# Neighbourhood attention by pairs of heads: scores in the two row halves of the array, value products alternating between its column halves

## The chip, the cores and the metric

The kernel runs on one core of a Trainium2 chip. The metric is the time of one execution on the device in microseconds. One core has five engines with a queue each: PE (TensorE, matrix products), DVE (VectorE), ACT (ScalarE), POOL (GpSimd) and SP, which issues the transfers. They meet through semaphores alone. PE's array has 128 rows (contraction) and 128 columns (output partitions); a product may use 64 of either.

## What is computed

A trunk of two layers over 512 latent tokens and 256 context tokens, width 1024. The even layer has, between two half feed-forward networks, a multi-scale pooling and a two-dimensional neighbourhood attention of 8 heads of 64, side by side; the odd layer has a recurrent block there. The part that matters here:

```python
def neighbourhood_attention(q, k, v, kc, vc, rpb):
    # q, k, v of the latent tokens on a grid of 8 x 64; kc, vc of the context
    ...
        s_loc = jnp.einsum('bjqhd,bkjchd->bhjqkc', qb, k_slab, preferred_element_type=F32) * NA_SCALE
        ...
        s_loc = jnp.where(mask6, s_loc + bias[None], -jnp.inf)
        s_ctx = jnp.einsum('bjqhd,bmhd->bhjqm', qb, kc, preferred_element_type=F32) * NA_SCALE
        s = jnp.concatenate([s_loc.reshape(B, H, n_cb, NB_COLS, n_loc), s_ctx], axis=-1)
        p = jax.nn.softmax(s, axis=-1).astype(v.dtype)
        ...
        o = (jnp.einsum('bhjqkc,bkjchd->bjqhd', p_loc, v_slab)
             + jnp.einsum('bhjqm,bmhd->bjqhd', p[..., n_loc:], vc))

def context_attention(q, k, v):
    s = jnp.einsum('bqhd,bkhd->bhqk', q, k, preferred_element_type=F32) * NA_SCALE
    p = jax.nn.softmax(s, axis=-1).astype(v.dtype)
    return jnp.einsum('bhqk,bkhd->bqhd', p, v)
```

The latent grid is cut into 4 column blocks of 16 columns. The 128 queries of a block (16 columns of 8 rows) see a slab of 32 columns, 256 keys, and the 256 context keys. The 256 context queries see the context keys.

## The kernel before

Everything is written out engine by engine, in the order in which each engine does it; semaphores count what is done. The attention is in float32, and a float32 product is two records on PE (a high and a low part of the weights); a transpose is one.

**Steps.** `STEPS` lists (h, j): 8 heads, and for each the 4 blocks (j < 4, 512 keys) and 2 tiles of context queries (j = 4, 5, 256 keys), 48 steps. For step s:
- PE `scores(s)` (lines 1799 to 1819): one product, the 128 queries as weights, the keys streaming. A head has 64 channels, so it uses 64 of the 128 rows: head h lies in half h % 2 of tile h // 2 of `q_t` and `k_t`. It writes one bank, half s % 2 of `pair_a`, and waits for `max_done` of step s - 2.
- DVE `lowest(s)` (L1439): adds the bias and takes the row's lowest value into `prob`, buffer s % 3 (scores are kept negated). ACT (L917): the exponential with its row sum. DVE `normalise(s)`: reciprocal (L1447), scaling (L1449).
- PE `turn(s)` (L1829): transposes the 4 (context: 2) tiles of 128 keys into half s % 2 of `pair_b`. ACT `copy_turned(s)` (L852) takes them into `prob_t`, buffer s % 2.
- PE `values(s)` (L1854): 4 (context: 2) products with 64 columns of values as weights, summed in `pair_c` (blocks) or `pair_r` (context queries), in the partitions of half h % 2 and in bank (h // 2) % 2, so that two pairs of heads have their own outputs.
- When both heads of pair t are done, DVE `take_heads(t)` (L1458, L1460) copies the 768 outputs to `mixed`, ACT `heads_high` (L911) and POOL `heads_low` (L676) split them into a high and a low part for the output projection, which is the next stage.

**Order.** PE: scores 0 and 1, and then in turn scores(s + 2), turn(s), values(s - 1). DVE: lowest(s), normalise(s - 1), and take_heads(t) in step j = 3 of the head after next. ACT: exponential(s), copy_turned(s - 1). POOL makes three bias tiles for a head (L692) in buffer h % 2, once the head two before no longer reads them, from tables which SP loads (L578).

The loop on PE, whose order stays:

```python
            scores(0)
            scores(1)
            for s in range(n):
                if s + 2 < n:
                    scores(s + 2)
                turn(s)
                if s >= 1:
                    values(s - 1)
            values(n - 1)
```

## Time and profile before

| | us |
|---|---|
| median of 3 runs | 2909.53 (2909.39 to 2911.92) |
| profiled execution | 2915.29 |
| its span, first to last instruction | 2913.5 |
| attention in it, first score product to first load of the next stage | 118.0 (831.24 to 949.20) |

The profile is of one execution. The windows of rows 2 leave out the first one, from 831.24 to 837.26; their sum row holds all three. A row of a timeline gives the start and how long the group lasts to the end of its last instruction, which overlaps the next one's start. Since products are pipelined, their own durations are latencies: what one costs PE is read from the distance between the starts of weight loads ("PEld"). A product over 64 rows reads 64\*128, one that makes 64 columns 128\*64. "issue" in brackets means that the engine waited for nothing but its own queue.

### The profile page before, as it was taken

Reading aid. Unit: us, or ns where it says so; the run is one execution under the profiler, and the core shown is the slowest. Engines: PE = TensorE matmul, PEld = TensorE weight load, DVE = VectorE, ACT = ScalarE, POOL = GpSimd, SP = SyncE. Lnnn points to the kernel's source line nnn. Section 1 sums busy time; section 2 is a strip of 40 time slices with the busy share of each in tenths; the row PEclk is TensorE's granted clock in tenths of the full one; section 3 lists DMA queues with packets and bytes.
Section 4 is the critical chain, followed back from the end, with each engine's and each line's share of the span. In section 5 each row is a group of like instructions: output and inputs, shape, how many; then the busy total and the mean of one; then the engine's idle time right before and its main releaser. Section 6 shows DMA issues by size and latency. Waiting matters only on the chain.

```text
span 2913.5 us, 40217 instructions
## 1 busy us (share of the span) xinstructions
PE 2767.8 (95%) x15161; PEld 2597.9 (89%) x15161; DVE 1485.7 (51%) x2553; ACT 772.6 (27%) x1039; POOL 896.8 (31%) x360
## 2 busy tenths in 40 slices
PE   6799999999999989999999999999998887899998
PEld 6799999998965989999999899999997775778887
DVE  5655555655535366655665523522238887432233
ACT  1322111112145232211111322111125665332222
POOL 0133222332222223322332223222223444244442
PEclk6899999999999999999999999999998997999999
DMA  5244334432210234434443122312211112223332
GB/s 197 58 127 129 111 101 126 127 100 69 68 61 19 65 88 115 123 100 116 115 123 107 44 65 80 107 58 61 75 52 40 55 54 57 70 86 107 88 101 79
DMA packets 413083, 256.77 MB, mean 88 GB/s; under 512 B 6653, under 2 KB 405846, under 8 KB 413014
## 3 DMA queue, kind: packets, MB, share of 16 engines
q1 hardware_dynamic: 413014, 255.87, 30.4%
q8 instruction: 40, 0.66, 0.1%
q14 instruction: 29, 0.24, 0.0%
HBM read 252.70 MB, written 4.25 MB: 88 GB/s over the span
## 4 chain that ended last, share of the span: by engine, by line
PE 65%; issue 19%; DVE 6%; POOL 5%; ACT 4%; DMA 0%; SPq 0%; POOLq 0%; DVEq 0%; ACTq 0%
PE pair_b L1575 28%; PE pair_a L1575 28%; POOL w_lo L647 5%; PE pair_c L1625 2%; PE pair_c L1854 1%; PE pair_a L1815 1%; DVE decay L1535 1%; PE pair_b L1829 1%; DVE decay L1533 1%; PE pair_a L1565 1%; DVE gate_i L1529 1%; DVE h_lo L1176 1%; DVE root L1527 1%; ACT decay L975 1%; ACT root L977 1%
## 5 line engine op out<-in xcount | busy, mean ns | idle before, releaser
L647 POOL TENSOR_TENSOR w_lo<-raw,w_hi 128x1024 fp32r<-128x1024 f32 (+3 forms) x302 | 829.5, 2748 | 1796.7 <-ACT w_hi L750 1796.7
L750 ACT ACTIVATE w_hi<-raw 128x1024 fp32r<-128x1024 f32 (+3 forms) x302 | 337.2, 1117 | 1281.1 <-PE pair_b L1575 443.7
L1067 DVE TENSOR_TENSOR work_g<-work_s,pair_b 128x768 f32<-128x768 f32 (+1 forms) x88 | 78.1, 888 | 702.2 <-PE pair_b L1575 539.7
L1037 DVE SCALAR_TENSOR_TENSOR ada_sums<-ada_raw,cvec,ada_sums 128x256 f32<-128x256 f32 x896 | 395.7, 515 | 0.0
L1575 PE MATMUL pair_a<-h_hi,w_hi 128*128 128x384 f32 x1312 | 338.3, 338 | 9.6 <-POOL w_lo L647 9.6
L1575 PE MATMUL pair_a<-h_lo,w_hi 128*128 128x384 f32 x1312 | 333.6, 335 | 0.0
L1575 PE MATMUL pair_a<-h_hi,w_lo 128*128 128x384 f32 x1312 | 333.6, 335 | 0.0
L1575 PE MATMUL pair_b<-h_hi,w_hi 128*128 128x384 f32 x1168 | 297.7, 335 | 5.9 <-POOL w_lo L647 5.9
L1575 PE MATMUL pair_b<-h_hi,w_lo 128*128 128x384 f32 x1168 | 297.6, 335 | 0.0
L1575 PE MATMUL pair_b<-h_lo,w_hi 128*128 128x384 f32 x1168 | 297.5, 335 | 0.0
L1575 PEld LDWEIGHTS pair_a<-h_hi,w_hi 128*128 128x128 f32 x1312 | 234.5, 189 | 13.5 <-issue 9.6
L1575 PEld LDWEIGHTS pair_a<-h_lo,w_hi 128*128 128x128 f32 x1312 | 237.5, 188 | 0.0
L1575 PEld LDWEIGHTS pair_a<-h_hi,w_lo 128*128 128x128 f32 x1312 | 237.5, 188 | 0.0
L1575 PEld LDWEIGHTS pair_b<-h_hi,w_hi 128*128 128x128 f32 x1168 | 211.7, 189 | 6.5 <-POOL w_lo L647 6.5
L1575 PEld LDWEIGHTS pair_b<-h_lo,w_hi 128*128 128x128 f32 x1168 | 211.9, 189 | 0.0
L1575 PEld LDWEIGHTS pair_b<-h_hi,w_lo 128*128 128x128 f32 x1168 | 211.9, 189 | 0.0
L1098 DVE SCALAR_TENSOR_TENSOR resid<-pair_b,mod_g,resid 128x512 f32<-128x512 f32 (+3 forms) x74 | 42.3, 603 | 314.4 <-PE pair_b L1575 245.2
L1565 PE MATMUL pair_b<-h_hi,w_hi 128*128 128x512 f32 (+3 forms) x352 | 140.0, 398 | 33.3 <-DVE gelu L1514 33.1
L1073 DVE TENSOR_TENSOR g_lo<-work_g,g_hi 128x768 f32 (+1 forms) x88 | 147.3, 1673 | 10.8
L1566 PE MATMUL pair_b<-h_lo,w_hi 128*128 128x512 f32 (+3 forms) x352 | 137.5, 391 | 0.0
L1565 PE MATMUL pair_a<-h_hi,w_hi 128*128 128x512 f32 (+2 forms) x280 | 115.7, 413 | 22.8 <-DVE h_lo L1176 19.2
L1567 PE MATMUL pair_b<-h_hi,w_lo 128*128 128x512 f32 (+3 forms) x352 | 136.8, 389 | 0.0
(272 smaller groups left out, 4548.5 us busy)
## 6 DMA issues: line engine op xcount, KB each, us to landing
raw<-in_ffn_w_gu_dram SPq DMA_DIRECT2D x176, 512.0 KB, 3.9
ada_raw<-in_ada_w_dram SPq DMA_DIRECT2D x64, 1024.0 KB, 5.2
raw<-in_ffn_w_down_dram SPq DMA_DIRECT2D x64, 704.0 KB, 5.5
raw<-in_rg_w_in_dram SPq DMA_DIRECT2D x20, 512.0 KB, 3.8
ada_first<-in_ada_w_dram SPq DMA_DIRECT2D x4, 2048.0 KB, 18.0
raw<-in_ab_w_in_dram SPq DMA_DIRECT2D x16, 512.0 KB, 3.8
raw<-in_rg_w_out_dram SPq DMA_DIRECT2D x8, 640.0 KB, 4.6
raw<-in_ab_w_out_dram SPq DMA_DIRECT2D x8, 512.0 KB, 4.1
```

The lines of the kernel that those rows point to most:

```text
L647: nc.gpsimd.tensor_tensor(wl[:, par, 0:kt * P], raw[:, par, 0:kt * P], wh[:, par, 0:kt * P].bitcast(F32), ALU.subtract).then_inc(split_rea ...
L750: nc.scalar.activation(wh[:, par, 0:kt * P], raw[:, par, 0:kt * P], ACT.Copy).then_inc(hi_done, 1)
L975: nc.scalar.activation(decay[d][:, :], gate_r[d][:, :], ACT.Exp, bias=rg_scale[:, m:m + 1], scale=rg_scale[:, m:m + 1])
L1037: step = nc.vector.scalar_tensor_tensor(out=sums[v], in0=tiles(k), scalar=c_k, in1=sums[v], op0=ALU.mult, op1=ALU.add)
L1067: nc.vector.tensor_tensor(gbuf[:, 0, 0:W], sbuf[:, 0, 0:W], up, ALU.mult)\
L1073: nc.vector.tensor_tensor(gl[:, ds(i, 1), 0:W].rearrange("p o n -> p (o n)"), gbuf[:, 0, 0:W], gh[:, ds(i, 1), 0:W].rearrange("p o n -> p ...
L1098: return nc.vector.scalar_tensor_tensor(out=resid[:, k, a:b], in0=src, scalar=mod_g[:, SITE[name], k, v:v + 1], in1=resid[:, k, a:b], op0= ...
L1565: nc.tensor.matmul(dst, w1, hi, start=start, stop=False)
L1566: nc.tensor.matmul(dst, w1, lo, start=False, stop=False)
L1567: return nc.tensor.matmul(dst, w2, hi, start=False, stop=stop)
L1575: last = nc.tensor.matmul(tokens(ps, a, a + HALF), w, of[:, k, a:a + HALF], start=begins, stop=ends)
L1625: last = nc.tensor.matmul(pC[:, 2 * t + v:2 * t + v + 1], ada_sum[:, v, t * P:(t + 1) * P], ones[:, 0:1], start=True, stop=True)
```

## The change

`STEPS` becomes 24 steps of (t, j), where t is a pair of heads. Each step does both heads a = 0, 1:
- scores: head 0's product in rows 0 to 63, then head 1's in rows 64 to 127, to the two halves of one double bank; double banks `pair_a` and `pair_b` alternate.
- turns: both heads' tiles, now to `pair_c`, half a. prob has 6 buffers, prob_t and `pair_c` one for each head, so turn(s, a) waits for copy(s - 1, a), and copy(s, a) for values(s - 1).
- values: for each tile of keys head 0's product and then head 1's, to partitions 0 to 63 and 64 to 127 of `pair_r`, blocks in its first bank and context queries in its second. There is one set of outputs: the first values of a pair wait for `heads_taken` of the pair before.
- DVE does lowest for both heads, then normalise for both of the step before; take_heads comes in the second step of the next pair (j == 1). ACT does two exponentials, then two copies; heads_high comes in the third step.
- POOL makes the bias tiles variant by variant for both heads, each as soon as the pair before no longer reads that variant.

```diff
-        prob = late("prob", [P, 3, 512])
+        prob = late("prob", [P, 3 * 2, 512])
...
-        STEPS = [(h, j) for h in range(HEADS) for j in range(BLOCKS + 2)]
+        STEPS = [(t, j) for t in range(KP) for j in range(BLOCKS + 2)]
+        PER_PAIR = BLOCKS + 2
+        def keys_of(j):
+            return NK + CTX if j < BLOCKS else CTX
+        def nth(s, a):
+            return 2 * s + a + 1
+        def stat(tile, s, a):
+            n = s % 4 * 2 + a
+            return tile[:, n:n + 1]
...
-                    sp.wait_ge(bias_done, h - 1)
+                    sp.wait_ge(bias_done, 3 * (h // 2))
...
-            for h in range(HEADS):
-                if h == 2:
+            def biases(t, v):
+                if v == 0:
+                    for a in range(2):
+                        pool.wait_ge(table_landed[a], 16 * (t + 1))
+                if t >= 1:
+                    last_use = max(j for j in range(BLOCKS) if VARIANT[j] == v)
+                    pool.wait_ge(max_done, nth(PER_PAIR * (t - 1) + last_use, 1))
+                for a in range(2):
+                    shifted = bass.AP(tensor=table[:, :, :].tensor, offset=table[:, a, SHIFT[v]:SHIFT[v] + 1].offset,
+                                      ap=[list(table[:, 0, 0:1].ap[0]), [1, SLAB], [RPB_C, GRID_R]])
+                    last = nc.gpsimd.tensor_tensor(bias[:, 3 * a + v, :].rearrange("p (c r) -> p c r", r=GRID_R),
+                                                   mask[:, v, :].rearrange("p (c r) -> p c r", r=GRID_R), shifted, ALU.subtract)
+                last.then_inc(bias_done, 1)
+            pool.wait_ge(mask_done, 1)
+            for t in range(KP):
+                if t == 1:
                     low(P_ABOUT, 0, KD)
                     low(P_ABOUT + 1, 1, KD)
-                pool.wait_ge(table_landed[h % 2], 16 * (h // 2 + 1))
-                pool.wait_ge(mask_done, 1)
-                if h >= 2:
-                    pool.wait_ge(max_done, (BLOCKS + 2) * (h - 2) + BLOCKS)
                 for v in range(3):
-                    t = bass.AP(tensor=table[:, :, :].tensor, offset=table[:, h % 2, SHIFT[v]:SHIFT[v] + 1].offset,
-                                ap=[list(table[:, 0, 0:1].ap[0]), [1, SLAB], [RPB_C, GRID_R]])
-                    last = nc.gpsimd.tensor_tensor(bias[:, h % 2 * 3 + v, :].rearrange("p (c r) -> p c r", r=GRID_R),
-                                                   mask[:, v, :].rearrange("p (c r) -> p c r", r=GRID_R), t, ALU.subtract)
-                last.then_inc(bias_done, 1)
-                if h in (3, 5, 7):
-                    heads_low(h // 2 - 1)
+                    biases(t, v)
+                if t >= 1:
+                    heads_low(t - 1)
...
-            def copy_turned(s):
-                j, b = STEPS[s][1], s % 2
-                W = NK + CTX if j < BLOCKS else CTX
-                act.wait_ge(turned_done, s + 1)
-                if s >= 2:
-                    act.wait_ge(pv_done, s - 1)
-                nc.scalar.activation(prob_t[:, b, 0:W], pB[:, b * 512:b * 512 + W], ACT.Copy).then_inc(prob_t_done, 1)
+            def copy_turned(s, a):
+                W = keys_of(STEPS[s][1])
+                act.wait_ge(turned_done, nth(s, a))
+                if s >= 1:
+                    act.wait_ge(pv_done, s)
+                nc.scalar.activation(prob_t[:, a, 0:W], pC[:, a * 512:a * 512 + W], ACT.Copy).then_inc(prob_t_done, 1)
...
-                if j == 5 and h % 2 == 0 and h >= 2:
-                    heads_high(h // 2 - 1)
-            copy_turned(len(STEPS) - 1)
+                    for a in range(2):
+                        copy_turned(s - 1, a)
+                if j == 2 and t >= 1:
+                    heads_high(t - 1)
+            for a in range(2):
+                copy_turned(len(STEPS) - 1, a)
...
             def take_heads(t):
-                dve.wait_ge(pv_done, (2 * t + 2) * (BLOCKS + 2))
+                dve.wait_ge(pv_done, PER_PAIR * (t + 1))
                 dve.wait_ge(mixed_split, KP + t - 1)
                 f = att_f[:, t % 2, :]
-                o, oc = pC[:, (t % 2) * 512:(t % 2) * 512 + SEQ], pR[:, (t % 2) * 512:(t % 2) * 512 + CTX]
+                o, oc = pR[:, 0:SEQ], pR[:, 512:512 + CTX]
...
-            for s, (h, j) in enumerate(STEPS):
-                lowest(s)
+            for s, (t, j) in enumerate(STEPS):
+                for a in range(2):
+                    lowest(s, a)
                 if s >= 1:
-                    normalise(s - 1)
-                if j == 3 and h % 2 == 0 and h >= 2:
-                    take_heads(h // 2 - 1)
-            normalise(len(STEPS) - 1)
+                    for a in range(2):
+                        normalise(s - 1, a)
+                if j == 1 and t >= 1:
+                    take_heads(t - 1)
+            for a in range(2):
+                normalise(len(STEPS) - 1, a)
...
             def scores(s):
-                h, j = STEPS[s]
-                t, a = divmod(h, 2)
-                rows = slice(a * DH, (a + 1) * DH)
-                b = s % 2
-                if s >= 2:
-                    pe.wait_ge(max_done, s - 1)
+                t, j = STEPS[s]
+                if s < 2:
+                    pe.wait_ge(proj_done, 2 + 16)
+                for a in range(2):
+                    rows = slice(a * DH, (a + 1) * DH)
+                    if s >= 2:
+                        pe.wait_ge(max_done, nth(s - 2, a))
+                    bank = pair[s % 2][:, a * 512:(a + 1) * 512]
+                    if j < BLOCKS:
+                        q = qT[rows, t, (BLOCKS - 1 - j) * P:(BLOCKS - j) * P]
+                        k0 = SLAB_AT[j] * GRID_R
+                        keys = bass.AP(tensor=kT[:, :, :].tensor, offset=kT[rows, t, k0:k0 + 1].offset,
+                                       ap=[list(kT[rows, t, 0:1].ap[0]), [SEQ - k0, 2], [1, NK]])
+                        bank = bank.rearrange("p (g n) -> p g n", n=NK)
+                    else:
+                        q, keys, bank = qT[rows, t, j * P:(j + 1) * P], kT[rows, t, SEQ:T], bank[:, 0:CTX]
+                    nc.tensor.matmul(bank, q, keys, start=True, stop=True).then_inc(scores_done, 1)
+            def turn(s, a):
+                pe.wait_ge(prob_scaled, nth(s, a))
+                if s == 0:
+                    pe.wait_ge(mixed_done, KP)
                 else:
-                    pe.wait_ge(proj_done, 2 + 16)
-                bank = pA[:, b * 512:(b + 1) * 512]
-                if j < BLOCKS:
-                    q = qT[rows, t, (BLOCKS - 1 - j) * P:(BLOCKS - j) * P]
-                    k0 = SLAB_AT[j] * GRID_R
-                    keys = bass.AP(tensor=kT[:, :, :].tensor, offset=kT[rows, t, k0:k0 + 1].offset,
-                                   ap=[list(kT[rows, t, 0:1].ap[0]), [SEQ - k0, 2], [1, NK]])
-                    last = nc.tensor.matmul(bank[:, :].rearrange("p (g n) -> p g n", n=NK), q, keys, start=True, stop=True)
-                else:
-                    q = qT[rows, t, j * P:(j + 1) * P]
-                    last = nc.tensor.matmul(bank[:, 0:CTX], q, kT[rows, t, SEQ:T], start=True, stop=True)
-                last.then_inc(scores_done, 1)
-            def turn(s):
-                h, j = STEPS[s]
-                b = s % 2
-                pe.wait_ge(prob_scaled, s + 1)
-                if s >= 2:
-                    pe.wait_ge(prob_t_done, s - 1)
-                for t in range(4 if j < BLOCKS else 2):
-                    last = nc.tensor.transpose(pB[:, b * 512 + t * P:b * 512 + (t + 1) * P],
-                                               prob[:, s % 3, t * P:(t + 1) * P], ident[:, :])
+                    pe.wait_ge(prob_t_done, nth(s - 1, a))
+                for i in range(keys_of(STEPS[s][1]) // P):
+                    last = nc.tensor.transpose(pC[:, a * 512 + i * P:a * 512 + (i + 1) * P],
+                                               prob[:, s % 3 * 2 + a, i * P:(i + 1) * P], ident[:, :])
                 last.then_inc(turned_done, 1)
             def values(s):
-                h, j = STEPS[s]
-                t, a = divmod(h, 2)
-                rows = slice(a * DH, (a + 1) * DH)
-                b = s % 2
-                pe.wait_ge(prob_t_done, s + 1)
+                t, j = STEPS[s]
+                pe.wait_ge(prob_t_done, nth(s, 1))
                 if s == 0:
                     pe.wait_ge(v_loaded, 16 * BLOCKS)
-                    pe.wait_ge(mixed_done, KP)
-                if j == 0 and a == 0 and t >= 2:
-                    pe.wait_ge(heads_taken, t - 1)
-                if j < BLOCKS:
-                    c0 = (t % 2) * 512 + (BLOCKS - 1 - j) * P
-                    dst = pC[rows, c0:c0 + P]
-                    tiles = [vslab[:, 2 * j, h * DH:(h + 1) * DH], vslab[:, 2 * j + 1, h * DH:(h + 1) * DH]]
-                else:
-                    dst = pR[rows, (t % 2) * 512 + (j - BLOCKS) * P:(t % 2) * 512 + (j - BLOCKS + 1) * P]
-                    tiles = []
-                tiles += [vtok[:, SEQ // P + i, h * DH:(h + 1) * DH] for i in range(2)]
+                if j == 0 and t >= 1:
+                    pe.wait_ge(heads_taken, t)
+                c0 = (BLOCKS - 1 - j) * P if j < BLOCKS else 512 + (j - BLOCKS) * P
+                tiles = [vslab[:, 2 * j, :], vslab[:, 2 * j + 1, :]] if j < BLOCKS else []
+                tiles += [vtok[:, SEQ // P + i, :] for i in range(2)]
                 for i, v in enumerate(tiles):
-                    last = nc.tensor.matmul(dst, v, prob_t[:, b, i * P:(i + 1) * P], start=(i == 0),
-                                            stop=(i == len(tiles) - 1))
+                    for a in range(2):
+                        h = 2 * t + a
+                        last = nc.tensor.matmul(pR[a * DH:(a + 1) * DH, c0:c0 + P], v[:, h * DH:(h + 1) * DH],
+                                                prob_t[:, a, i * P:(i + 1) * P], start=(i == 0), stop=(i == len(tiles) - 1))
                 last.then_inc(pv_done, 1)
...
-                turn(s)
+                for a in range(2):
+                    turn(s, a)
                 if s >= 1:
                     values(s - 1)
```

PE, a context step's turns and values between two block steps' scores, before (one head; names with buffer numbers, ident_63 is the identity, pair_a the score banks, pair_b the turned, pair_r and pair_c the outputs):

```order
L1815 MATMUL pair_a<-k_t_83,q_t_82 128x512 [waits max_done]
L1829 MATMUL pair_b<-ident_63,prob_85 128x128 [waits prob_t_done,prob_scaled]
L1829 MATMUL pair_b<-ident_63,prob_85 128x128
L1854 MATMUL pair_r<-prob_t_88,v_tokens_80 64x128 [waits prob_t_done]
L1854 MATMUL pair_r<-prob_t_88,v_tokens_80 64x128
L1815 MATMUL pair_a<-k_t_83,q_t_82 128x512 [waits max_done]
```

and after, the same place of the second pair:

```order
L1840 MATMUL pair_b<-k_t_83,q_t_82 128x512 [waits max_done] x2
L1849 MATMUL pair_c<-ident_63,prob_85 128x128 [waits prob_t_done,prob_scaled]
L1849 MATMUL pair_c<-ident_63,prob_85 128x128
L1849 MATMUL pair_c<-ident_63,prob_85 128x128 [waits prob_t_done,prob_scaled]
L1849 MATMUL pair_c<-ident_63,prob_85 128x128
L1867 MATMUL pair_r<-prob_t_88,v_tokens_80 64x128 [waits prob_t_done]
L1867 MATMUL pair_r<-prob_t_88,v_tokens_80 64x128 x3
L1840 MATMUL pair_a<-k_t_83,q_t_82 128x512 [waits max_done] x2
```

Every shape now comes twice in a row, once for each head, and only then does PE go to the next shape.

DVE around the copies of a finished pair's outputs, before (ISA is `lowest`):

```order
L1439 ISA prob,neg_max<-pair_a,bias 128x512 [waits scores_done,turned_done]
L1439 ISA neg_max 128x1
L1447 RECIPROCAL row_inv<-row_sum 128x1 [waits prob_done]
L1449 TENSOR_SCALAR prob<-prob,row_inv 128x512 [waits inv_done]
L1458 COPY mixed<-pair_c 128x512 [waits mixed_split,pv_done]
L1460 COPY mixed<-pair_r 128x256
L1439 ISA prob,neg_max<-pair_a,bias 128x256 [waits scores_done,turned_done]
L1439 ISA neg_max 128x1
```

and after:

```order
L1467 RECIPROCAL row_inv<-row_sum 128x1 [waits prob_done]
L1469 TENSOR_SCALAR prob<-prob,row_inv 128x512 [waits inv_done]
L1478 COPY mixed<-pair_r 128x512 [waits mixed_split,pv_done]
L1480 COPY mixed<-pair_r 128x256
L1460 ISA prob,neg_max<-pair_a,bias 128x512 [waits scores_done,turned_done,bias_done]
L1460 ISA neg_max 128x1
L1460 ISA prob,neg_max<-pair_a,bias 128x512 [waits scores_done,turned_done,bias_done]
L1460 ISA neg_max 128x1
L1467 RECIPROCAL row_inv<-row_sum 128x1 [waits prob_done]
L1469 TENSOR_SCALAR prob<-prob,row_inv 128x512 [waits inv_done]
```

The copies moved from the fourth step of the head after next to the second step of the next pair, right behind the last values that they wait for; two lowest and two scalings are queued behind them.

## Rows read from the trace of the kernel before

**Rows 1.** The page's busy times: us, share of the span, instructions.
```profile
PE 2767.8 (95%) x15161; PEld 2597.9 (89%) x15161; DVE 1485.7 (51%) x2553; ACT 772.6 (27%) x1039; POOL 896.8 (31%) x360
```

**Rows 2.** Windows: length, busy PE, PEld, DVE, ACT, POOL, granted clock, DMA.
```profile
837.26:847.50 10.24, 10.24 (x33) 6.44 (x33) 3.17 (x12) 3.68 (x9) 2.75 (x3) 0.50 0.05 14
847.50:949.20 101.70, 101.47 (x538) 59.70 (x537) 55.65 (x180) 53.80 (x134) 19.00 (x18) 1.00 0.06 15
sum 117.96, PE 115.01 PEld 67.29 DVE 63.13 ACT 62.83 POOL 21.75; mean PE 38.34 PEld 22.43 DVE 21.04 ACT 20.94 POOL 7.25
```

**Rows 3.** Timeline of PE's weight loads, one head: start, length, instruction.
```profile
863.25 0.29 PEld L1815 LDWEIGHTS pair_a<-k_t,q_t 64*128 64x128 f32 x2 [0.17 <-issue]
864.30 0.20 PEld L1829 LDWEIGHTS pair_b<-ident,prob 128*128 128x128 f32 x2 [0.76 <-issue]
864.67 0.41 PEld L1854 LDWEIGHTS pair_c<-prob_t,v_slabs 128*64 128x64 f32 x4 [0.17 <-issue]
...
868.74 0.42 PEld L1829 LDWEIGHTS pair_b<-ident,prob 128*128 128x128 f32 x4 [0.76 <-DVE prob L1449]
869.33 0.41 PEld L1854 LDWEIGHTS pair_r<-prob_t,v_tokens 128*64 128x64 f32 x4 [0.17 <-issue]
869.91 0.29 PEld L1815 LDWEIGHTS pair_a<-k_t,q_t 64*128 64x128 f32 x2 [0.17 <-issue]
...
871.55 0.41 PEld L1854 LDWEIGHTS pair_c<-prob_t,v_slabs 128*64 128x64 f32 x4 [0.17 <-issue]
...
872.57 0.29 PEld L1818 LDWEIGHTS pair_a<-k_t,q_t 64*128 64x128 f32 x2 [0.17 <-issue]
873.19 0.42 PEld L1829 LDWEIGHTS pair_b<-ident,prob 128*128 128x128 f32 x4 [0.33 <-issue]
...
877.03 0.18 PEld L1815 LDWEIGHTS pair_a<-k_t,q_t 64*128 64x128 f32 x1 [0.17 <-issue]
```

**Rows 4.** Timeline of the start, all engines.
```profile
831.24 1.98 PE L1815 MATMUL pair_a<-k_t,q_t 64*128 64x512 f32 x4
...
834.75 0.68 DVE L1439 CUSTOM_DVE_ANT_1 prob<-pair_a,bias 128x512 f32<-128x512 f32 x1
835.36 0.08 DVE L1439 DVE_READ_ACCUMULATOR2_ANT neg_max<- 128x1 f32 x1
...
835.50 1.12 PE L1815 MATMUL pair_a<-k_t,q_t 64*128 64x512 f32 x2 [2.28 <-DVE neg_max L1439]
...
836.33 0.16 DVE L1447 RECIPROCAL row_inv<-row_sum 128x1 f32<-128x1 f32 x1 [0.27 <-ACT prob L917]
836.53 0.49 DVE L1449 TENSOR_SCALAR prob<-prob,row_inv 128x512 f32<-128x512 f32 x1
...
837.07 0.98 PE L1829 MATMUL pair_b<-ident,prob 128*128 128x128 f32 x4 [0.45 <-DVE prob L1449]
```

**Rows 5.** Weight loads of value products: the first two together, and min/median/max ns.
```profile
862.23 0.19 PEld L1854 LDWEIGHTS pair_c<-prob_t,v_slabs 128*64 128x64 f32 x2 [0.17 <-issue]
...
L1854 PEld LDWEIGHTS pair_c<-prob_t,v_slabs x128: 132/137/231, 841.0 to 947.0; 128*64 128x64 f32 x128
```

**Rows 6.** Groups by form, 834 to 950: busy us, mean ns of one, idle before.
```profile
L917 ACT ACTIVATE prob<-prob,neg_max 128x512 f32<-128x512 f32 x32 | 22.9, 716 | 1.5 <-DVE neg_max L1439 0.3
...
L852 ACT ACTIVATE prob_t<-pair_b 128x512 f32<-128x512 f32 x32 | 19.1, 598 | 35.8 <-PE pair_b L1829 35.8
...
L676 POOL TENSOR_TENSOR h_lo<-mixed,h_hi 128x768 fp32r<-128x768 f32 x3 | 5.4, 1813 | 56.1 <-ACT h_hi L911 56.1
...
L1458 DVE COPY mixed<-pair_c 128x512 f32<-128x512 f32 x4 | 2.7, 686 | 2.2 <-PE pair_r L1854 2.2
...
L1460 DVE COPY mixed<-pair_r 128x256 f32<-128x256 f32 x4 | 1.7, 416 | 0.0
```

**Rows 7.** Timeline where POOL makes bias tiles beside a scaling.
```profile
881.52 2.67 POOL L692 TENSOR_TENSOR bias<-mask,rpb_table 128x256 f32<-128x256 f32 x3
881.56 1.10 DVE L1449 TENSOR_SCALAR prob<-prob,row_inv 128x512 f32<-128x512 f32 x1
```

56 lines of the change are left out of this document (27 added, 29 removed).

## The prediction

> **What bounds the kernel now.** I read first the page's busy shares, then the windows of the attention stage, then the weight loads of one head in it, the timeline of its start, and its groups by form. PE is busy for 95% of the span [rows 1]. The change touches one stage alone: from the first score product at 831.24 to the first load of the output projection at 949.20, 118.0 us, in which PE is busy 115.0, DVE 63.1 and ACT 62.8 us [rows 2]. Before and behind it nothing moves, so its gain or loss is that of the kernel as long as the stage behind finds its weights split and its heads ready, which I come to.
>
> In the steady part PE sets the pace. A head takes 877.03 - 863.25 = 13.78 us [rows 3]. Read the distances between loads: a block's scores 1.05 (863.25 to 864.30), a context block's 0.62 (872.57 to 873.19), four turns 0.59 (868.74 to 869.33), two turns 0.37 (864.30 to 864.67), eight value records 1.02 (871.55 to 872.57), four 0.58 (869.33 to 869.91) [rows 3]. With 4 blocks and 2 context blocks a head: 4 x (1.05 + 0.59 + 1.02) + 2 x (0.62 + 0.37 + 0.58) = 13.78. The head is PE's own work to the last 0.01 us; eight heads are 110.2. The other 7.8 us of 118.0 are the start (below).
>
> (2) The halves. Head 0's scores are followed by head 1's in the other rows and another bank, and value products go to alternating column halves. Before, neighbours are always in one half, so no row shows whether two halves stream at once. Bounds: not at all (0.43 and 0.11 each, as now), or as far as two records of one half can't overlap. In the order a-high, a-low, b-high, b-low the second of head 0 and the first of head 1 then run together: 3 times instead of 4 for a pair of scores, and 2k+1 instead of 4k for k tiles of values. I take the full overlap: the operands, the output banks or partitions and the weights are all disjoint, and two 64-column loads with the product between them start 0.055 apart [rows 5], so issue and loading can feed a record every 0.055 us. Nearest rows for a gain are those of one half, which is the other end of the range.
>
> The Trainium skill, "TensorEngine Tiling (Array Packing)", section Key Properties, says that tiles load and multiply in parallel and that only a change of mode drains the array; by it I would take this same end, and by the rows alone either. The Trainium skill, "TensorE: Matmul & The Clock Gate", Part 3, says on the other hand that a load overlaps running matmuls only when its row group differs. Value products all use all rows, so by it the loads would be exposed. This trace speaks against it: eight value records come at 0.11 us each with their loads hidden [rows 3]. If it held between column halves, two overlapped records would cost 0.11 + 2 x 0.055 = 0.22, as much as now, and only the scores would gain.
>
> With full overlap a block step is scores 0.19 + 3 x 0.43 = 1.48, turns 0.15 + 8 x 0.11 = 1.03, values 0.14 + 9 x 0.11 = 1.13: 3.64. A context step is 0.84 + 0.59 + 0.69 = 2.12. A pair: 4 x 3.64 + 2 x 2.12 = 18.8, four pairs 75.2 us, where 110.2 stood.
>
> (3) Do DVE and ACT keep up? Per block step DVE does for two heads lowest 0.61 (834.75 to 835.36), reciprocal and scaling 0.20 + 0.49 (836.33 to 837.02): 2.6 us; ACT two exponentials at 0.72 and two copies at 0.60: 2.6 [rows 4, 6]. Both are below 3.64, and a context step needs about 1.7 of 2.12. Copies: the turned bank and prob_t are now single, so turn(s, a) waits for copy(s-1, a), which waits for values(s-2). While PE does scores (1.48), the first copy (0.60 and a hand-over of 0.1) ends; at context scores (0.84) by 0.1 us only. Free, but without slack.
>
> (4) The new wait. pair_r now holds one pair's outputs instead of two. take_heads stands in DVE's order behind normalise(6t+6) and waits for the last values of pair t. Behind it are queued lowest(6t+8), both heads, and normalise(6t+7), for which PE's turn(6t+7) waits. From the end of those values: 0.1 + 1.10 for the two copies [rows 6] + 1.22 for two lowest + 0.69 = 3.1; PE meanwhile has only the next scores, 1.48. A wait of 1.6, with an echo of 0.1, at three boundaries: 5.1 us. Before, take_heads came steps later and hid.
>
> (5) The end: after the last scores nothing covers the chain. The two copies after values(22) stand bare (0.9), and the last two context steps' exponentials and scalings, now two heads deep, cost some 1.6: 2.5 us.
>
> (6) The start. Scores 0 wait in the bank until DVE comes free at 834.75; turn 0 came at 837.07. Now four lowest stand ahead: 834.75 + 4 x 0.61 + 0.69 = 837.9. Against the same schedule without that delay this is 1.9 us. Then the clock: after PE's waits of 2.28 and 0.45 [rows 4] the granted clock was 0.50 for 10.24 us [rows 2], the lower level, 1.2 GHz of 2.4; with PE bound that costs 5.1. With overlap PE waits about as long (until 835.5, and from 837.1 to 837.9), so I keep 5.1.
>
> (7) POOL. Bias tiles are the same 24, asked for variant by variant. While three of them run (2.67), a scaling takes 1.10 [rows 7] instead of 0.49 [rows 4], and PE's next turn is behind it. With less slack I add 1.5, two or three such cases. Order: once heads_high has ended, in a pair's third step, heads_low (1.81) and the first variant's two tiles (2 x 0.9) [rows 6, 7] take 3.6, and by the step times above the next pair's first lowest comes some 5 us after; free, and if not it costs 1 or 2 us a pair. SP's table loads wait for bias tiles of a pair earlier and have a whole pair's time. Behind the stage the last heads take the same chain, and the POOL splits of the next panels follow it as before: nothing.
>
> **Sum**: 75.2 + 5.1 + 2.5 + 1.9 + 5.1 + 1.5 = 91.3 against 118.0: 26.7 us less. The profiled execution took 2915.29 (span 2913.5), which becomes 2888.6; the median of the runs, 5.76 lower, 2909.53, becomes 2882.8. If the clock holds at the start, 2877.7.
>
> **Rivals.**
> A. *Halves take turns.* Against it only the disjointness; for it, that no row shows two products at once. A block step is 1.91 + 1.03 + 1.90 = 4.84, a context step 2.66: a pair 24.7, all 98.7. Plus boundaries 3 x 1.3, end 2.5, start 1.0, POOL 0.5, and 0 to 5.1 of clock: 106.6 to 111.7, so 2898 to 2903; 2900.5.
> B. *Overlap in part*: the load of the other half starts only when the first half's last record does, or values gain nothing (the rule above), or the bare hand-overs of (3) cost 0.3 to 0.5 a step. A scores pair 1.59, a four-tile couple of values 0.32 instead of 0.22 a tile: a pair 21.3, 10 us more than the forecast in all; values without gain give 15 more. 2888 to 2898; 2893.
> C. *Each change of half drains, as a change of shape does*, 0.145 a time. There are 7 in a block's values, 3 in a context block's and 1 in scores: 16 x 7 + 8 x 3 + 24 = 160, so 23 us on top of A: 2921 to 2926, slower; 2923. It turns the sign from 0.04 to 0.07 us a change on. For it: the drain of 0.09 in every fixed part. Against: it comes with a new shape, and here the shape stays.
> D. *The pairs don't change PE's bound*: some other new wait in DVE, POOL or the tables eats the gain of A; within 5 us of 2909.5.
>
> **How the numbers follow.** Forecast 0.46, A 0.22, B 0.21, C 0.07, D 0.04. About 0.2%, 5.8 us, is what a measurement can tell here. Faster: the forecast, B and nine tenths of A, 0.87; the same: the slow end of A and most of D, 0.05; slower: C and a little of D, 0.08. The range of eight in ten, 2876 to 2903, holds the forecast with the clock held or fallen, B and A.
>
> **What would show it.** Scores: four records whose second and third start together and a group of 1.48, not 1.91. Values: 16 records in 1.13, not 1.90 (0.055 or 0.11 apart), or 2.9 under C. A pair of 18.8 plus one wait at a boundary, PE's turn waiting for DVE's scaling behind the two mixed copies. The clock at 0.50 for some 10 us near 837. Wrong would be a wait in every step for copies or scalings, a lowest waiting for bias, or a gain that shows in the stage and not in the span.

## The result and the profile after

| | before | after |
|---|---|---|
| median of 4 runs | 2910.31 (2909.39 to 2911.92) | 2877.55 (2877.28 to 2879.45) |
| profiled execution | 2915.29 | 2877.64 |
| its span | 2913.5 | 2875.9 |
| attention in it | 117.96 (831.24 to 949.20) | 84.63 (828.51 to 913.14) |

The ratio of the times is 0.9889, with a 95% interval of 0.9873 to 0.9905: 1.1% faster, 32.8 us between the medians. The two profiled executions differ by 37.7: 33.3 in the attention stage, 2.7 ahead of it and 1.6 behind it. What lies ahead of the stage took 828.5 us after and 831.2 before, what lies behind it 1962.7 and 1964.3. Over all executions below these two are 826.2 to 833.6 and 1960.6 to 1964.0, whatever stands in the stage, so totals of single executions scatter by some us, and the length of the stage is the better measure.

The page's busy times of after, beside [rows 1]:

```profile
PE 2719.7 (95%) x15161; PEld 2569.5 (89%) x15161; DVE 1487.4 (52%) x2553; ACT 768.7 (27%) x1039; POOL 891.1 (31%) x360
```

PE is busy 48 us less with the same 15161 instructions. DVE, ACT and POOL are within 6 us of what they were. The windows of the stage, columns as in [rows 2]:

```profile
828.51:833.40 4.89, 2.62 (x12) 1.00 (x11) 3.48 (x8) 4.47 (x7) 0.00 (x0) 1.00 0.00 0
833.40:840.22 6.82, 6.77 (x20) 3.36 (x19) 6.50 (x17) 4.88 (x14) 3.52 (x4) 0.50 0.01 4
840.22:913.14 72.92, 61.52 (x550) 38.44 (x548) 53.99 (x178) 49.78 (x133) 18.11 (x17) 1.00 0.08 23
sum 84.63, PE 70.91 PEld 42.81 DVE 63.96 ACT 59.13 POOL 21.63; mean PE 23.64 PEld 14.27 DVE 21.32 ACT 19.71 POOL 7.21
```

PE had been busy for 115.0 of 118.0 us; now it is for 70.9 of 84.6, and DVE, at 64.0, is not far from it. The part at a granted clock of 0.50 is 6.8 us instead of 10.24.

A step with block scores, a context step's turns and block values: weight loads on PE, with the product row of its scores last (compare [rows 3]):

```profile
847.83 0.30 PEld L1840 LDWEIGHTS pair_a<-k_t,q_t 64*128 64x128 f32 x4 [0.17 <-issue]
848.89 0.52 PEld L1849 LDWEIGHTS pair_c<-ident,prob 128*128 128x128 f32 x4 [0.76 <-issue]
849.57 0.42 PEld L1867 LDWEIGHTS pair_r<-prob_t,v_slabs 128*64 128x64 f32 x8 [0.17 <-issue]
849.96 0.47 PEld L1867 LDWEIGHTS pair_r<-prob_t,v_tokens 128*64 128x64 f32 x8
850.60 0.30 PEld L1840 LDWEIGHTS pair_b<-k_t,q_t 64*128 64x128 f32 x4 [0.17 <-DVE neg_max L1460]
...
847.83 1.13 PE L1840 MATMUL pair_a<-k_t,q_t 64*128 64x512 f32 x4
```

The four loads of two heads' scores take 0.30 us, and the next shape follows 1.06 behind the first (847.83 to 848.89). One head alone took 1.05. So two block products cost what one did: the halves overlap not in part but wholly. Values: 16 records from 849.57 to 850.60 in 1.03, where 8 took 1.02. (The turns between them are those of a context step: 849.57 - 848.89 = 0.68, of which four turns are 0.59, and 0.09 is a wait.)

The boundary of a pair, PE's weight loads:

```profile
855.62 0.30 PEld L1840 LDWEIGHTS pair_b<-k_t,q_t 64*128 64x128 f32 x4 [0.17 <-issue]
858.63 0.42 PEld L1849 LDWEIGHTS pair_c<-ident,prob 128*128 128x128 f32 x4 [2.71 <-DVE prob L1469]
...
860.84 0.30 PEld L1840 LDWEIGHTS pair_a<-k_t,q_t 64*128 64x128 f32 x4 [0.17 <-issue]
861.73 0.91 PEld L1849 LDWEIGHTS pair_c<-ident,prob 128*128 128x128 f32 x8 [0.59 <-DVE prob L1469]
863.83 0.30 PEld L1840 LDWEIGHTS pair_b<-k_t,q_t 64*128 64x128 f32 x4 [0.17 <-issue]
865.07 0.42 PEld L1849 LDWEIGHTS pair_c<-ident,prob 128*128 128x128 f32 x4 [0.94 <-DVE prob L1469]
...
867.69 0.30 PEld L1840 LDWEIGHTS pair_a<-k_t,q_t 64*128 64x128 f32 x4 [0.17 <-issue]
...
875.49 0.30 PEld L1840 LDWEIGHTS pair_b<-k_t,q_t 64*128 64x128 f32 x4 [0.17 <-issue]
...
903.54 0.30 PEld L1840 LDWEIGHTS pair_b<-k_t,q_t 64*128 64x128 f32 x4 [0.17 <-issue]
```

and the other engines there:

```profile
855.75 0.69 DVE L1478 COPY mixed<-pair_r 128x512 f32<-128x512 f32 x1 [1.35 <-PE pair_r L1867]
...
861.01 1.09 ACT L872 ACTIVATE prob_t<-pair_c 128x512 f32<-128x512 f32 x2 [2.09 <-PE pair_r L1867]
...
861.99 0.84 ACT L931 ACTIVATE h_hi<-mixed 128x768 fp32r<-128x768 f32 x1
...
862.91 1.82 POOL L690 TENSOR_TENSOR h_lo<-mixed,h_hi 128x768 fp32r<-128x768 f32 x1 [20.02 <-ACT h_hi L931]
863.57 0.16 DVE L1467 RECIPROCAL row_inv<-row_sum 128x1 f32<-128x1 f32 x1 [1.10 <-ACT prob L938]
863.76 1.25 DVE L1469 TENSOR_SCALAR prob<-prob,row_inv 128x512 f32<-128x512 f32 x1
```

At the start of the stage, DVE's first `lowest` and the first of its rows there with idle time:

```profile
832.02 0.68 DVE L1460 CUSTOM_DVE_ANT_1 prob<-pair_a,bias 128x512 f32<-128x512 f32 x1
...
839.65 0.69 DVE L1460 CUSTOM_DVE_ANT_1 prob<-pair_b,bias 128x512 f32<-128x512 f32 x1 [0.18 <-PE pair_b L1840]
```

Between the two it works without a pause, and PE waits for it (2.27 us ahead of scores 2 at 832.77). Now the steady part. A step is the stretch from one scores' load to the next, named by the turns in it; the boundary is that of a pair's second step. A pair takes 19.87 us (855.62 to 875.49) and the next one 19.85, 19.86 on average. PE's own work for a pair, from distances between loads in which nothing is waited for, is 4 x 3.10 + 2 x 1.79 = 15.98, where 3.10 is 1.05 + 1.03 + 1.03 but for rounding and 1.79 is 0.62 + 0.59 + 0.58. So a pair holds 3.88 of waits. DVE stands idle 1.35 for the last values of a pair, copies them, and only then does the two lowest and the scaling that PE's turn waits for: this step takes 5.22 (855.62 to 860.84; 5.21 at the next two boundaries) instead of 3.10. The third takes 2.99 (860.84 to 863.83) instead of 0.62 + 1.03 + 1.03 = 2.68: turns wait for the copies out of the single bank. (The row of the turns at 861.73 names DVE's scaling, but head 0's had ended at 860.99; the first of ACT's two copies, which began at 861.01, ends some 0.1 ahead of the turns.) The fourth takes 3.86 (863.83 to 867.69) instead of 2.68: ACT does heads_high (0.84) ahead of the exponentials, DVE's reciprocal waits 1.10 for them, and the scaling behind it, for which PE's turns wait, takes 1.25 instead of 0.49 while POOL runs heads_low. The rest, 0.26, lies in three steps.

### The profile page after: what moved, and what is told of

Same layout as the page of the kernel before. It is cut to its first block, busy times and chain, and to the rows that moved or that the text cites. A ratio compares the mean times of both kernels' runs of the same rounds, so it can differ in the third digit from the quotient of the medians.

```text
span 2875.9 us, 40218 instructions
## 1 busy us (share of the span) xinstructions
PE 2719.7 (95%) x15161; PEld 2569.5 (89%) x15161; DVE 1487.4 (52%) x2553; ACT 768.7 (27%) x1039; POOL 891.1 (31%) x360
## 4 chain that ended last, share of the span: by engine, by line
PE 64%; issue 20%; DVE 7%; POOL 5%; ACT 4%; DMA 0%; SPq 0%; POOLq 0%; DVEq 0%; ACTq 0%
PE pair_b L1598 29%; PE pair_a L1598 28%; POOL w_lo L661 5%; PE pair_c L1648 2%; DVE decay L1558 1%; DVE decay L1556 1%; DVE h_lo L1199 1%; PE pair_c L1849 1%; DVE gate_i L1552 1%; PE pair_a L1588 1%; DVE root L1550 1%; ACT root L1000 1%; ACT decay L998 1%; DVE ada_sums L1060 1%; PE pair_r L1867 1%
## 5 line engine op out<-in xcount | busy, mean ns | idle before, releaser
L1096 DVE TENSOR_TENSOR g_lo<-work_g,g_hi 128x768 f32 (+1 forms) x88 | 161.5, 1835 | 10.8
## 6 DMA issues: line engine op xcount, KB each, us to landing
ada_first<-in_ada_w_dram SPq DMA_DIRECT2D x4, 2048.0 KB, 17.9
```

The source lines that it names most:

```text
L1096: nc.vector.tensor_tensor(gl[:, ds(i, 1), 0:W].rearrange("p o n -> p (o n)"), gbuf[:, 0, 0:W], gh[:, ds(i, 1), 0:W].rearrange("p o n -> p ...
```

## The experiments

Unless one says otherwise, a kernel is the changed one with the edit shown. "Stage" is the time from the first score load to the first load of the next stage. The half-clock stretches (granted clock 0.50, TensorE at 1.2 GHz) inside it are given with it, since they differ between executions of one kernel.

| kernel | time, median | before, same chip | stage | stretches at 0.50 |
|---|---|---|---|---|
| changed | 2877.55 | 2910.31 | 84.6 | 6.8 at the start |
| changed, again (e12) | 2880.41 | 2911.46 | 86.5 | 6.8 start, 3.4 last boundary |
| values by head (e1) | 2883.04 | 2910.12 | 93.6 | 6.8 start, 3.4 at two boundaries |
| scores in one half (e2) | 2890.61 | 2910.12 | 94.9 | 10.2 start |
| values in one half (e3) | 2897.10 | 2910.12 | 101.6 | 3.4 start, 3.4 at two boundaries |
| both in one half (e4) | 2905.98 | 2910.12 | 106.9 | none |
| the same, again (e11) | 2903.76 | 2911.46 | 111.3 | 3.4 at three boundaries |
| copies a step later (e5) | 2872.20 | 2910.67 | 78.6 | 3.4 start |
| no bias tiles (e6) | 2877.18 | 2910.67 | 87.0 | 6.8 start, 3.4 at two boundaries |
| both of these (e8) | 2874.97 | 2910.67 | 78.4 | 6.8 start |
| filler at the start (e7) | 2878.13 | 2910.67 | 85.3 | 3.4 last boundary |
| later, heads_high in step 5, bias tiles first (e9) | 2877.43 | 2911.46 | 82.4 | 3.4 start |
| later, heads_high in step 4 (e10) | 2875.42 | 2909.50 | 79.6 | 6.8 start |

The medians are of ten runs for "both in one half", of four where a ratio stands below, and else one run. The four runs of "changed, again" lie 5.3 us apart, so single runs that differ by less are not told apart by their times; there the steps of the trace carry the argument.

### Do the halves stream at once?

Three kernels keep the order and the waits of the change and take away one thing, the halves. *Scores in one half* (e2):

```diff
-                    rows = slice(a * DH, (a + 1) * DH)
+                    rows = slice(0, DH)
```

> The changed kernel, with both heads' score products taken from head 0's 64 rows (head 1's scores are head 0's, so head 1 is not computed). Theory, only the difference of rows lets the two run together: four records of a block step go from 1.05 to 0.19 + 4 x 0.43 = 1.91 us, context ones from 0.62 to 1.05; a pair's own work goes up by 4 x 0.86 + 2 x 0.43 = 4.3, less what it covers of the wait at the boundary and for scalings: the stage 92 to 98 from 84.6. Rival, the different banks are enough: no change.

Weight loads of one pair of block scores:

```profile
852.47 0.29 PEld L1840 LDWEIGHTS pair_a<-k_t,q_t 64*128 64x128 f32 x2 [0.17 <-issue]
853.01 0.19 PEld L1840 LDWEIGHTS pair_a<-k_t,q_t 64*128 64x128 f32 x1 [0.24 <-issue]
853.44 0.19 PEld L1840 LDWEIGHTS pair_a<-k_t,q_t 64*128 64x128 f32 x1 [0.24 <-issue]
854.38 0.42 PEld L1849 LDWEIGHTS pair_c<-ident,prob 128*128 128x128 f32 x4 [0.76 <-issue]
```

The four loads are now 0.43 apart from the second on, and the group lasts 1.91 (852.47 to 854.38), the price for no overlap; with two halves it was 1.06. Nothing but the rows differs.

*Values in one half* (e3):

```diff
-                        last = nc.tensor.matmul(pR[a * DH:(a + 1) * DH, c0:c0 + P], v[:, h * DH:(h + 1) * DH],
-                                                prob_t[:, a, i * P:(i + 1) * P], start=(i == 0), stop=(i == len(tiles) - 1))
+                        last = nc.tensor.matmul(pR[0:DH, c0:c0 + P], v[:, h * DH:(h + 1) * DH],
+                                                prob_t[:, a, i * P:(i + 1) * P], start=(i == 0 and a == 0),
+                                                stop=(i == len(tiles) - 1 and a == 1))
```

> The changed kernel, with both heads' value products summed into partitions 0 to 63 (the outputs of the two heads are added and the upper half is not computed). Theory, only the difference of column halves lets them run together: a block's 16 value records go from 1.03 to 0.14 + 16 x 0.11 = 1.90 us, a context step's 8 from 0.58 to 1.02; a pair 4 x 0.87 + 2 x 0.44 = 4.4 longer, less what it hides of waits: the stage 94 to 101. Rival: no change.

```profile
847.80 0.85 PEld L1867 LDWEIGHTS pair_r<-prob_t,v_slabs 128*64 128x64 f32 x8 [0.17 <-issue]
...
849.70 0.30 PEld L1840 LDWEIGHTS pair_b<-k_t,q_t 64*128 64x128 f32 x4 [0.17 <-issue]
```

Sixteen records take 1.90 (847.80 to 849.70) instead of 1.03. The stage of 101.6 lies just above the expected 94 to 101; its clock fell at two boundaries, which took 7.61 and 7.58 where the third took 6.07. Both edits at once (e4), and the same kernel once more (e11):

> The changed kernel with both of these: scores of both heads from head 0's rows, values of both into partitions 0 to 63 (so head 1 is not computed and the outputs are added). What is left of the change is that both heads are done behind each other in each shape of the array: half the changes of shape, and the waits of the single buffers. By the steps of the prediction (rival A): a pair 24.7, the stage 106 to 112, the kernel 2898 to 2903. If changes of shape cost nothing: a pair 27.6 as before, and slower than before by the boundary waits, 2912 to 2918.

> e4 once more, for a second trace: its first profiled execution had the stage at 106.9 with the clock at 1.00 throughout, while its timed runs spread from 2899 to 2912. Theory: the spread comes from whether the clock falls in the waits of the start and of the boundaries, which here costs PE time, because PE is the bound: the same step times (a pair 25.1), and up to 5 us more in the stage where a stretch at 0.50 shows. Rival: the stage is 106.9 again and the spread lies elsewhere.

Windows of the stage, first of e4, then of e11 (the third number from the end is the granted clock, 1.00 against 0.95):

```profile
829.43:936.34 106.91, 99.91 (x577) 67.34 (x576) 65.20 (x201) 59.44 (x152) 21.57 (x21) 1.00 0.06 16
```

```profile
829.48:940.80 111.32, 104.31 (x577) 71.42 (x576) 65.17 (x201) 59.44 (x152) 21.57 (x21) 0.95 0.06 15
```

With both halves taken away the stage is 106.9 us. That is what the prediction had worked out for rival A with the clock held (106.6), and the pair takes 25.87 (862.73 to 888.60) where A had 24.7 + 1.3. So the prices of grouping were right. What grouping alone is worth is less than the 11 us between the stages of before and e4, for before had its clock at 0.50 for 10.24 us: its three steps from 837.98 to 849.47 took 11.49 where the same steps of a later head take 7.12. With these 4.4 taken off, grouping gives at most some 7 us of stage, and in the time it isn't told from nothing: ratio 0.9991 (0.9981 to 1.0001), with runs from 2899.43 to 2911.71. The profiled execution, 2899.43, is the fastest of the ten and has the clock at 1.00 throughout its stage. In the second run the clock fell at each of the three boundaries, and each then took 7.54 instead of 6.07:

```profile
862.79 0.29 PEld L1840 LDWEIGHTS pair_b<-k_t,q_t 64*128 64x128 f32 x2 [0.17 <-issue]
...
870.33 0.73 PEld L1840 LDWEIGHTS pair_a<-k_t,q_t 64*128 64x128 f32 x4 [0.17 <-issue]
```

The two profiled executions differ by 4.4 us in the stage, as much as in the whole time (2899.43 and 2903.76). That the slower ones of e4's ten runs have more such stretches is likely and not shown, as they have no profile. Their mean granted clocks over the whole kernel go that way, 0.970 and 0.971 for the two fastest and 0.966 for the three slowest; but three fallen boundaries cost 4.4, and the ten runs spread over 12.3, so most of the spread lies outside the stage.

*Values by head* (e1) asks how much the order within the values matters:

```diff
-                for i, v in enumerate(tiles):
-                    for a in range(2):
+                for a in range(2):
+                    for i, v in enumerate(tiles):
```

> The changed kernel, with all value products of head 0 before all of head 1 instead of alternating; the work and the result are the same. In the changed kernel a block's 16 value records take 1.03 us and the attention stage 84.6. Theory 1, a product of the other half can start only when it is at most about one record behind in the queue: only the records at the joint run together, 15 of 0.11 + 0.14 = 1.8 us for a block's values, a pair 3 us longer, the stage 92 to 95. Theory 2, each half has a queue of its own that runs ahead: values stay at 1.03 and the stage at 84.6.

Products on PE, one block's values (head 0's eight records are queued first, then head 1's):

```profile
846.28 0.65 PE L1867 MATMUL pair_r<-prob_t,v_slabs 128*64 128x128 f32 x4
...
846.94 0.27 PE L1867 MATMUL pair_r<-prob_t,v_slabs 128*64 128x128 f32 x1
846.99 0.27 PE L1867 MATMUL pair_r<-prob_t,v_tokens 128*64 128x128 f32 x1
...
847.26 0.60 PE L1867 MATMUL pair_r<-prob_t,v_tokens 128*64 128x128 f32 x4
847.79 0.70 PE L1840 MATMUL pair_a<-k_t,q_t 64*128 64x512 f32 x2
```

The group takes 1.51 (846.28 to 847.79), between 1.03 and 1.90. Head 0's first four records run alone, its last four (tokens) share the array with head 1's first four (slabs), 0.05 apart, and head 1's last four run alone: 12 times 0.11 and the fixed 0.14 are 1.46. Records of head 1 start ahead of head 0's last ones, which stand before them in the queue. So a record may overtake earlier ones that wait for their half, but here by some four records only, and alternating, as the change does, is what puts all 16 side by side. Neither theory had this: the first gave 1.8 for the group, the second 1.03. That the stage of 93.6 fits the first one's 92 to 95 is chance, since its clock fell at two boundaries.

The Trainium skill, "TensorEngine Tiling (Array Packing)", section Key Properties, says that different tiles load and multiply in parallel and that a change of mode drains the array. The traces agree with the first, with 1.06 against 1.91 for scores and 1.03 against 1.90 for values. The Trainium skill, "TensorE: Matmul & The Clock Gate", Part 3, says in its list of what overlaps that a load overlaps running products only when its row group differs (its text above the list adds a load into the background weights), and that products start and end in the order of the program. Here value products all use the same rows and their loads cost nothing (1.03 for 16), which the list excludes, and e1's records of head 1 start ahead of earlier queued ones; the measurement decides. On the order of ends nothing is shown.

### What holds the boundary?

*Copies a step later* (e5): take_heads stands behind normalise of the third step instead of the second.

```diff
-                if j == 1 and t >= 1:
+                if j == 2 and t >= 1:
                     take_heads(t - 1)
```

> The changed kernel, with take_heads in the third step of the next pair (j == 2), behind the two lowest and the two scalings that were queued behind it. Theory: these no longer wait for the pair's last value products, and PE's wait of 1.95 us before the second step's turns goes at three boundaries; take_heads itself is done while PE does scores and turns: 4 to 6 us less than the changed kernel, the stage 79 to 81. Rival: the time comes back at the next wait for a scaling, since DVE is busy for 8 of 10 us; less than 2 us.

PE's loads and DVE's copy at the first boundary, and PE's load a pair later:

```profile
854.60 0.30 PEld L1840 LDWEIGHTS pair_b<-k_t,q_t 64*128 64x128 f32 x4 [0.17 <-DVE neg_max L1460]
...
855.70 0.68 DVE L1478 COPY mixed<-pair_r 128x512 f32<-128x512 f32 x1
857.88 0.30 PEld L1840 LDWEIGHTS pair_a<-k_t,q_t 64*128 64x128 f32 x4 [0.17 <-issue]
...
872.52 0.30 PEld L1840 LDWEIGHTS pair_b<-k_t,q_t 64*128 64x128 f32 x4 [0.17 <-DVE neg_max L1460]
```

The boundary step takes 3.28 (854.60 to 857.88) instead of 5.21. DVE no longer stands before the copy (no idle time in its row), and the turns are no longer late (the next scores come in 3.28). The pair takes 17.92, the stage 78.56, 6.1 less than the changed kernel's, of which three boundaries are 3 x 1.93 = 5.8. The whole time falls by about as much: 2872.20 (2867.44 to 2874.28), ratio to before 0.9864 (0.9847 to 0.9880), 5 us less than the changed kernel. The interval still touches the changed kernel's (0.9873 to 0.9905), but each of these four runs is below each of the changed kernel's eight (2876.62 and more). This is the best of the versions that leave nothing out.

### What holds the fourth step?

*No bias tiles* (e6): from the second pair on POOL writes one column of each tile instead of the 256.

```diff
                 for a in range(2):
+                    if t >= 1:
+                        last = nc.gpsimd.tensor_tensor(bias[:, 3 * a + v, 0:1], mask[:, v, 0:1], mask[:, v, 0:1], ALU.subtract)
+                        continue
                     shifted = bass.AP(
```

> The changed kernel without POOL's bias tiles from the second pair on (one column each is written in their place, so the bias of later pairs is left out). Theory: POOL's tiles beside DVE's scalings stretch these from 0.49 to 0.9 to 1.25 us, and PE waits 1.2 us a pair for them in the step before the context queries, and some at the start: the stage 3 to 5 us shorter, no scaling over 0.6. Rival, the scalings are late for another reason: less than 1 us.

Scalings on DVE in e6's stage (count: min/median/max ns), and the one ahead of the first fourth step's turns:

```profile
L1472 DVE TENSOR_SCALAR prob<-prob,row_inv x48: 352/486/1253, 832.9 to 910.1; 128x512 f32<-128x512 f32 x32, 128x256 f32<-128x256 f32 x16
...
862.37 1.25 DVE L1472 TENSOR_SCALAR prob<-prob,row_inv 128x512 f32<-128x512 f32 x1
```

Of 48 scalings 3 take over 600 ns, 1.25 each and all beside heads_low, where the changed kernel has 14. But the fourth step goes only from 3.86 to 3.47: 0.39 a pair. The other long scalings had cover. So POOL's bias tiles cost some 1 us in the stage, and not the 3 to 5 expected. The stage of 87.0 is no counter-evidence: its clock fell at two boundaries, where 6.55 and 6.68 stand instead of 5.21.

Together with the later copies (e8) PE should come to its own 15.98 a pair, or stay above it:

> take_heads in the third step and no bias tiles from the second pair on (their bias is left out). Theory: with both waits gone a pair costs PE's own work, 4 x 3.10 + 2 x 1.79 = 16.0 us, instead of 19.9; the stage about 73 to 75. Rival, DVE (2.6 us a block step, 14.8 a pair with take_heads) in its chain with ACT is the next bound: 17 to 18 a pair.

The pair takes 17.52, in steps of 3.28, 2.98, 3.47, 2.77, 2.23 and 2.79, against an own work of 3.10, 2.68, 2.68, 2.67, 2.22 and 2.66. So the expected 16.0 a pair and a stage of 73 to 75 were missed (78.4), and the rival's 17 to 18 came. With bias tiles gone and take_heads later, 0.8 stays in the fourth step and 0.3 in the third. Two things are left ahead of the fourth step's turns: heads_high on ACT, in front of the exponentials, and heads_low on POOL, beside the scaling.

*heads_high a step later than that* (e10, on top of e5):

```diff
-                if j == 2 and t >= 1:
+                if j == 3 and t >= 1:
                     heads_high(t - 1)
...
-                if j == 1 and t >= 1:
+                if j == 2 and t >= 1:
                     take_heads(t - 1)
```

> e5 with ACT's heads_high in the fourth step (j == 3) instead of the third, POOL's order as in the changed kernel. Of PE's wait of 1.18 us before the fourth step's turns 0.79 stays when no bias tiles are made (e8), and heads_high (0.84) stands there ahead of the exponentials whose scalings those turns wait for. Theory: ACT's 0.84 is that 0.79, and it goes; POOL's tiles come 3 us later and may be late for the next pair's first lowest by 0 to 1: a pair 17.1 to 17.9 and the stage 76 to 78.6. Rival, as in e9 the tiles only meet other scalings: a pair of 18 or more.

Its scores' loads from the one ahead of the fourth step's turns on, and why the later ones are late:

```profile
865.67 0.30 PEld L1840 LDWEIGHTS pair_b<-k_t,q_t 64*128 64x128 f32 x4 [0.17 <-issue]
868.66 0.30 PEld L1840 LDWEIGHTS pair_a<-k_t,q_t 64*128 64x128 f32 x4 [0.17 <-issue]
872.02 0.30 PEld L1840 LDWEIGHTS pair_b<-k_t,q_t 64*128 64x128 f32 x4 [0.17 <-DVE neg_max L1460]
...
871.33 0.69 DVE L1460 CUSTOM_DVE_ANT_1 prob<-pair_a,bias 128x512 f32<-128x512 f32 x1 [0.75 <-POOL bias L705]
```

The fourth step falls from 3.86 to 2.99 (865.67 to 868.66), so the split of the heads was what held it. Which half of it, this run can't say, since heads_low waits for heads_high and moved with it: the scaling ahead of these turns (864.87) has neither ACT's 0.84 before it nor POOL beside it, and takes 0.49. The changed kernel's rows say that it took both. There the scores ahead of the turns end at 864.45 (863.83 + 0.62) and the stretched scaling at 865.01 (863.76 + 1.25); at its usual 0.49 it would have ended at 864.25, in time, although heads_high had made it late. No run moves one half alone. And POOL's bias tiles, behind heads_low, come later too; the next pair's first lowest now waits 0.75 for them, and the next steps are 3.36 and 2.97 instead of 2.77 and 2.23. The pair takes 18.2, more than e5's 17.9 and the expected 17.1 to 17.9. The gain was given back to POOL's queue.

*heads_high in the fifth step, and POOL's order turned so that bias tiles come first* (e9):

```diff
-                if t >= 1:
-                    heads_low(t - 1)
+                if t >= 2:
+                    heads_low(t - 2)
+            heads_low(KP - 2)
...
-                if j == 2 and t >= 1:
+                if j == 4 and t >= 1:
                     heads_high(t - 1)
```

(with take_heads later, as in e5)

> e5 (take_heads in the third step), and in addition ACT's heads_high in the fifth step (j == 4) instead of the third, with POOL's heads_low moved behind the bias tiles of the next pair so that these don't wait for it. In e5 heads_high (0.84 us) and heads_low beside the scalings stand before the fourth step's turns, where PE still waits 1.2 us. Theory: that wait goes, a pair 16.7 to 17.2 instead of 17.9, the stage 75.5 to 77.5 instead of 78.6. Rival: POOL's tiles and splits stretch the same number of scalings in another step, and the stage stays within 1 us of 78.6.

```profile
860.50 1.87 POOL L705 TENSOR_TENSOR bias<-mask,rpb_table 128x256 f32<-128x256 f32 x2 [3.19 <-DVE neg_max L1461]
860.53 1.11 DVE L1470 TENSOR_SCALAR prob<-prob,row_inv 128x512 f32<-128x512 f32 x1
```

A miss. The stage is 82.4, 3.9 longer than e5's where 1 to 3 less was expected; the ratio to before, 0.9880 (0.9863 to 0.9896), is above e5's 0.9864, with intervals that overlap. The bias tiles now run as soon as their variant is free, which is beside the block steps' scalings, where DVE has no slack: 18 scalings take over 600 ns, as the 1.11 above. The boundary step is 4.32 and the one after 3.94 (e5: 3.28 and 2.98). So bias tiles beside scalings go with 0.4 us a pair in one place and 2 in another. That the 2 are all POOL's is argued from the rows; no run turns POOL's order alone.

### What does the clock cost?

*Filler at the start* (e7) keeps PE busy while it waits there; the filler's results are overwritten:

```diff
+            def filler(k):
+                for _ in range(k):
+                    nc.tensor.matmul(pC[:, 0:512], ident[:, :], kT[:, 0, 0:512], start=True, stop=True)
+            pe.wait_ge(mixed_done, KP)
+            filler(2)
             for s in range(n):
                 if s + 2 < n:
                     scores(s + 2)
+                if s == 0:
+                    filler(1)
```

> The changed kernel with three products on PE that nobody reads (identity by 512 keys into the turned bank), two before scores 2 and one before the first turns, to fill the wait in which the clock falls to 0.50 for 6.8 us from 833.4 on. Theory 1, the clock costs half of that, 3.4 us, as the prediction took it: 3 us less. Theory 2, DVE and not PE sets the pace at the start (it is busy without a gap from 832.0 to 839.4): with the clock at 1.00 less than 1 us is won, or some is lost to the fillers.

```profile
829.69:841.00 11.31, 9.88 (x37) 4.09 (x37) 9.76 (x24) 9.35 (x19) 3.54 (x4) 1.00 0.00 1
```

```profile
856.57 0.30 PEld L1840 LDWEIGHTS pair_b<-k_t,q_t 64*128 64x128 f32 x4 [0.17 <-issue]
```

The clock is 1.00 at the start. Yet the tenth step's scores come 26.88 us behind the first (829.69 to 856.57), where they came 27.11 behind in the changed kernel (828.51 to 855.62): 6.8 us at half clock cost 0.2. In e12, where the stretch comes 6.0 us behind the first scores instead of 4.9, it is 27.6, so 0.7. The fillers hide no price of their own here, for e5, without them and with 3.4 us at half clock, has 26.88 as well (827.72 to 854.60). DVE sets the pace there, busy 9.76 of the 11.31 us. The ratio is 0.9884 (0.9868 to 0.9901), that of the change.

*The changed kernel once more* (e12), for the spread:

> The changed kernel itself, beside the runs above on the same chip, so that e5 and e9 have their comparison: 2877 to 2879, the stage 84.6 with a stretch at 0.50 near the start and perhaps one at a boundary (in e7 and e6, whose waits there are the same, such a stretch came and cost about 0.9).

```profile
893.54 0.30 PEld L1840 LDWEIGHTS pair_b<-k_t,q_t 64*128 64x128 f32 x4 [0.17 <-issue]
...
900.09 0.49 PEld L1840 LDWEIGHTS pair_a<-k_t,q_t 64*128 64x128 f32 x4 [0.33 <-issue]
```

```profile
897.12:900.53 3.41, 3.41 (x23) 2.72 (x24) 2.31 (x8) 0.26 (x1) 0.00 (x0) 0.50 0.00 0
```

The median, 2880.41, is above the expected 2877 to 2879, and the ratio, 0.9894 (0.9878 to 0.9911), is the first one's. Here the clock fell at the last boundary, which took 6.55 (893.54 to 900.09) instead of 5.21: 3.4 us at half clock cost 1.34, where PE has nothing to wait for. At the start twice that stretch cost 0.2 to 0.7. The profiled execution is the fastest of its four (2876.62) in spite of a stage of 86.5, so 2 us of stage don't show in a single time.

## Why the prediction was right, and where it was not

It gave 2882.8 with a range of 2876 to 2903 and the forecast "full overlap"; 2877.55 came. The gain was 32.8 us where 26.7 stood. The stage was put at 91.3 us and took 84.6, 6.7 less. The profiled execution came 11.0 below its 2888.6, 6.7 of it in the stage and 4.3 outside it; it stands only 0.1 above its median, where 5.8 had been carried over from before, and so the median is off by 5.3. That these partly cancel is luck. Its terms:

| step | predicted | measured |
|---|---|---|
| four pairs, PE's own work | 75.2 | 4 x 15.98 = 63.9 |
| three boundaries | 5.1 | 3 x (2.11 + 0.31) = 7.3 |
| start and clock | 1.9 + 5.1 | 6.9 |
| end | 2.5 | 3.5 |
| POOL, fourth step | 1.5 | 2 x 1.18 = 2.4 |
| other steps | 0 | 2 x 0.26 = 0.5 |
| sum | 91.3 | 84.5 |

**(1) Grouping** was right. With the halves taken away the stage is 106.9 (e4), 0.3 from the 106.6 worked out for it, and the fixed parts go as counted. (That e11's 111.3 meets the upper end of 111.7 is chance: the clock fell at three boundaries there, and not at the start.)

**(2) The halves: the mis-sized term.** The sum took the order a-high, a-low, b-high, b-low and let b's first record run beside a's second, "3 times instead of 4" for scores and "2k+1 instead of 4k" for values. In fact b's first record starts beside a's first: four score records last 1.13 (847.83) where [rows 4] had 1.12 for one head's two. A block's scores are 1.05, not 1.48, and values 1.03, not 1.13. A block step is 3.10 instead of 3.64, a context step 1.79 instead of 2.12, and four pairs are 11.3 us less. What failed was the assumption that a record waits for all that are ahead of it in the queue. It waits for its own half, and e1 shows that one can pass some four others on the way.

**(3) Copies and hand-over**: held to be free "but without slack". The third step of a pair waits 0.31, since its turns (861.73) come 0.27 later than the scores of a context step allow (860.84 + 0.62). With shorter scores that slack was gone. A rival had 0.3 to 0.5 in every step for this; it is so in one step in six.

**(4) The boundary** is the mechanism that was predicted, at its place: DVE stands for the last values, and two lowest and a scaling are queued behind the copies. It costs 2.11 instead of 1.6, for the scores that hide a part of it are 0.43 shorter (1.05 for 1.48). e5 removes 1.93 of it with one moved line.

**(5) The end** holds 3.5: from the last scores' load at 903.54 to 913.14 are 9.60, of which PE's own work is 0.62 + 1.03 + 1.03 + 0.59 + 1.03 + 0.59 + 0.58 + 0.58 = 6.05. The term was 2.5. The copies ahead of the last values stand bare as predicted (0.9; from 911.08 + 0.58 to the load at 912.55). The rest is 2.6 instead of 1.6; in it lies the last fourth step, whose turns come 0.62 late (904.78 instead of 903.54 + 0.62), which the term left out. With the split a step later (e10) the end takes 9.32 (902.07 to 911.39), 0.28 less. What makes the remainder is open.

**(6) Start and clock: right sum, wrong reasons.** The first 27.1 us hold 20.2 of PE's own work, so 6.9 of waits against 7.0 predicted. But the clock's 5.1 was worked out for a bound PE. DVE worked through from 832.02, with its first idle time at 839.65, and e7 puts the clock's share at 0.2 (0.7 in e12). What fills the stretch is DVE's first steps, two heads deep, which the term of 1.9 had far too small. Without e7 the match would have passed for a proof.

**(7) POOL**: 1.5 stood for scalings stretched by bias tiles, and 0.39 for each of two pairs is 0.8 (e6). The other 0.79 of the fourth step's wait is the split of the heads, which no term had: heads_high's 0.84 on ACT stands ahead of two exponentials that DVE needs at once, and heads_low on POOL stretches the scaling behind them by 0.76. e10, which moves both, has 0.87 less in that step. The share of each is open.

Of the rivals, A (halves take turns) would have been e4, B (in part) e1 for the values alone, and C (each change of half drains) is refuted by 16 records with 15 changes of half in 1.03 us. D's new wait in DVE is there, 2.2 us more in the stage than foreseen, where the halves give 22.

**Where the gain is from.** Before 118.0 (clock fallen at the start, some 4.4 of it); grouping 106.9 (clock held) to 111.3 (fallen at three boundaries); the row halves on top of it 101.6; the column halves instead 94.9; both 84.6 to 86.5. PE's own work fell by 4 x (27.56 - 15.98) = 46.3, but only 33.3 reached the stage, since waits of 20.7 stand where 7.8 did, and 4.4 of these 7.8 were the clock's. 28% of what PE saved was lost to them, and e5 gets back 6 us.

## What to carry to other kernels

Where a product fills half of the array, put the other half's product right behind it in the queue, product by product: here the second came free, and with the value products queued by whole heads half of their gain went. After such a cut, look at once for what was hidden behind the old streaming: a copy queued ahead of the softmax on DVE and a split queued ahead of the exponentials on ACT, with its other half on POOL beside the scaling, had cost nothing, and became 2 and 0.9 us a pair. A match in the sum proves no term of it; take the term away and see.

## What the runs showed of the hardware

- Two float32 products in the two row halves (64 x 128 weights, 512 columns) cost 1.06 us together, one alone 1.05; 16 value records in two column halves 1.03, 8 in one 1.02. The same products in one half take 1.91 and 1.90.
- Each half has its own order: a product whose half is free starts ahead of earlier queued ones of the other half, by about four records (e1: 4 alone, 4 beside 4, 4 alone, 1.51 us).
- A stretch at half clock costs what PE's part in the bound is: 0.2 to 0.7 us for 6.8 at the start, where DVE sets the pace, and 1.3 to 1.5 for 3.4 at a boundary. Whether it comes differs between executions of one kernel (e4 none and e11 three; the changed kernel one or two).
- While POOL runs a two-operand subtraction, DVE's scaling of 128 x 512 goes from 0.49 to 0.90 to 1.25 us. `lowest`, which reads its scores from the accumulators' banks, stays at 0.69 beside it (871.33 in e10).
